# A sixth buffer for expert weights in a decoder layer's mixture of experts

## What is computed

```python
h = rmsnorm(x, norm_mix_g) * (1 + sc_a) + sh_a            # shifts, scales, gates from silu(c) @ ada_w
g_q, g_k, g_v, g_g, g_a, s_q, s_k, s_v = split(h @ w_in)   # 2320 columns
o_gla = gla_mixer(...)        # 4 heads, chunked gated linear attention
o_swa = swa_sink_mixer(...)   # 8 q / 2 kv heads, window 128, rotary, sinks
x = x + gt_a * (concat(o_gla, o_swa) @ w_out)
h = rmsnorm(x, norm_ffn_g) * (1 + sc_f) + sh_f
# router: top-1 of 4 groups, then top-2 of 8 experts inside it; 32 experts
y = sum over the two experts of weight * ((silu(h @ w_gate) * (h @ w_up)) @ w_down)   # D_EXPERT = 256
x = rmsnorm(x + gt_f * y, final_norm_g)
```

## Time and profile before

| | us |
|---|---|
| median of 3 runs | 602.33 (602.03 to 610.63) |
| the profiled execution | 603.5 |
| its span, first to last instruction | 601.6 |
| TensorE busy | 497.2 (83% of the span) |
| VectorE (DVE) busy | 272.7 (45%) |
| ScalarE (ACT) busy | 146.3 (24%) |
| GpSimd (POOL) busy | 80.4 (13%) |
| mean DMA rate over the span | 271 GB/s |

### The profile page before, as it was taken

The page is one execution under the profiler, slowest core; times in us unless marked ns, Lnnn a source line. Parts: engine busy times, 40 slices in busy tenths (PEclk is TensorE's granted clock), DMA queues, the critical chain, the costliest instruction groups (busy, mean ns, idle before and its releaser), DMA issues.

```text
span 601.6 us, 6875 instructions
## 1 busy us (share of the span) xinstructions
PE 497.2 (83%) x2596; PEld 286.6 (48%) x2596; DVE 272.7 (45%) x653; ACT 146.3 (24%) x368; POOL 80.4 (13%) x128
## 2 busy tenths in 40 slices
PE   0497999999999998999848999988898776889800
PEld 0453584646565654455545555544454443444300
DVE  4588919395665746455532623222221220222256
ACT  2402214332544532202213212111111110111111
POOL 5000000000000000012122222222212220221111
PEclk9999999999999999999958999999988898899955
DMA  8997966924500035600079999999999999999373
GB/s 295 378 354 234 352 243 215 344 71 166 114 1 1 1 115 230 285 35 36 35 268 352 382 415 415 417 413 416 415 416 417 420 416 413 416 417 373 130 288 140
DMA packets 51099, 163.10 MB, mean 271 GB/s; under 512 B 10301, under 2 KB 11342, under 8 KB 42618
## 3 DMA queue, kind: packets, MB, share of 16 engines
q1 hardware_dynamic: 40632, 151.10, 65.1%
q0 software_dynamic: 5312, 8.48, 3.8%
q10 hardware_dynamic: 5122, 3.08, 1.7%
HBM read 158.63 MB, written 12.91 MB: 285 GB/s over the span
## 4 chain that ended last, share of the span: by engine, by line
PE 59%; DMA 21%; SPq 8%; DVE 6%; issue 2%; ACT 1%; ACTq 1%; POOL 0%; POOLq 0%; DVEq 0%
PE ps L1383 19%; DMA ring<-in_w_up 17%; PE ps L1648 10%; PE ps L1562 9%; PE ps L1662 4%; SPq L458 3%; SPq L462 2%; DMA xres<-in_x 2%; SPq L459 1%; PE ps L1588 1%; ACTq L703 1%; PE ps L1640 1%; PE ps L1428 1%; PE ps L1494 1%; PE ps L1485 1%
## 5 line engine op out<-in xcount | busy, mean ns | idle before, releaser
L1383 PE MATMUL ps<-ring,hreg 128*128 128x512 f32 (+1 forms) x320 | 130.4, 562 | 2.1 <-DVE hreg L980 2.1
L1648 PE MATMUL ps<-ring,proj 128*64 128x256 f32 x336 | 87.0, 418 | 19.2 <-DMA ring<-in_w_up 18.6
L1383 PEld LDWEIGHTS ps<-ring,hreg 128*128 128x128 f32 x320 | 60.5, 193 | 62.0 <-issue 57.5
L1649 PE MATMUL ps<-ring,proj 128*64 128x256 f32 x336 | 87.0, 418 | 0.0
L1300 DVE TENSOR_TENSOR proj<-proj,ps 64x256 f32<-64x256 f32 x33 | 14.0, 423 | 159.7 <-ACT proj L880 159.7
L1648 PEld LDWEIGHTS ps<-ring,proj 128*64 128x64 f32 x336 | 48.7, 150 | 47.9 <-DMA ring<-in_w_up 19.5
L951 DVE SCALAR_TENSOR_TENSOR wide<-wide,csil 128x512 f32<-128x512 f32 x72 | 49.2, 747 | 2.3 <-DMA wide<-in_ada_w 2.2
L880 ACT ACTIVATE proj<-ps 64x256 f32<-64x256 f32 x33 | 12.4, 376 | 153.8 <-PE ps L1649 153.8
L1649 PEld LDWEIGHTS ps<-ring,proj 128*64 128x64 f32 x336 | 48.7, 150 | 0.0
L636 POOL DMA_INDIRECT y_rows<-proj,hreg x33 | 32.9, 997 | 116.0 <-DVE proj L1306 116.0
L1662 PE MATMUL ps<-ring,proj 128*64 128x512 f32 x168 | 40.2, 599 | 0.4 <-ACT proj L884 0.4
(11 more groups left out here) (277 smaller groups left out, 699.4 us busy)
## 6 DMA issues: line engine op xcount, KB each, us to landing
wide<-in_ada_w SPq DMA_DIRECT2D x24, 1024.0 KB, 8.7
ring<-in_w_gate SPq DMA_DIRECT2D x21, 1024.0 KB
ring<-in_w_up SPq DMA_DIRECT2D x21, 1024.0 KB
ring<-in_w_down SPq DMA_DIRECT2D x21, 1024.0 KB, 23.4
wide<-in_w_down SPq DMA_DIRECT2D x12, 1024.0 KB, 24.3
ring<-in_w_in SPq DMA_DIRECT2D x4, 2048.0 KB, 9.6
wide<-in_w_gate SPq DMA_DIRECT2D x6, 1024.0 KB
wide<-in_w_up SPq DMA_DIRECT2D x6, 1024.0 KB
```

The lines of the kernel that those rows point to most:

```text
L1383: mm = pe.matmul(ps[bank_of(st)][:, 0:CW[ch]], hT[:, k, b * P:(b + 1) * P], win_sb[ch][:, k, :], start=k == 0, stop=k == KD - 1)
L1648: pe.matmul(ps[bank][0:TILE, 0:F], hx[:, k, :], wg_sb[w][:, k, :], start=k == 0, stop=k == KD - 1)
L1649: mm = pe.matmul(ps[bank][TILE:P, 0:F], hx[:, k, :], wu_sb[w][:, k, :], start=k == 0, stop=k == KD - 1)
```

## The change

A sixth set of weight buffers, number 3 (`MIXED`), takes experts 3, 9, 15, 21 and 27. The former sets 3 and 4 become 4 and 5. The new set has no tensor of its own:

- gate lies in `proj` columns CQ:CV, up in CG:CA, each as 4 pieces of 512 columns (2 KB) a partition;
- down lies in `proj` columns CSK:WIN (4 pieces of 256 columns), in `gla_g` (512 columns) and in the second half of `gt_f` (512 columns), which nothing used; its load is three transfers in place of one.

Expert 3's load is issued after that of expert 2, when the four `gate_scale` and all copies of the projection are done, ahead of the wait for the output projection. Experts 4 and 5 take the places at which 3 and 4 were issued, and the loop starts at n = 6.

The working buffers make room: `heT` goes to columns CV:CG of `proj` (the mixer's result), `eo` to CSQ:CSK, the hidden values and masks to `turned`, `hg` to `spare` and to a part of `hreg`. Both last ones are in use until later than the old place was, so POOL clears them after its walk through MIXER_ORDER, behind the last squares of norm2 and the last router logits. The ids' operand `named` goes from `gla_g` to a `wa2_` of 128 rows, and `fin_g` from `spare` to `wide`, whose load waits for `e_down` of 32.

```diff
-SLOTS = 5
+SLOTS = 6
+MIXED = 3
...
-        wa2 = sb("wa2", [RANK + 1, GH * DK])
-        fin_g = spare
+        wa2_ = sb("wa2", [P, GH * DK])
+        wa2 = wa2_[0:RANK + 1, :]
+        fin_g = wide[:, 0:D]
...
+        heads = [proj[:, :, CQ:CV], proj[:, :, CG:CA]]
+        tails = [proj[:, :, CSK:WIN], gla_g[:, :], gt_f[:, D // 2:D]]
+        part += [heads]
         part += [[wide[:, a * PART:(a + 1) * PART] for a in range(3)]]
         part += [[hreg[:, 0:PART], early[:, :], wide[:, 3 * PART:4 * PART]]]
...
+        def w_cols(u, a, k):
+
+            if u == MIXED:
+                return heads[a][:, k // 2, (k % 2) * F:(k % 2 + 1) * F]
+            return part[u][a][:, k * F:(k + 1) * F]
+
+        def wd_cols(u, f, i):
+
+            if u == MIXED:
+                return tails[0][:, 2 * i:2 * i + 2, :] if f == 0 else tails[1 + i]
+            return part[u][2][:, f * D + i * PC:f * D + (i + 1) * PC]
+
+        def wd_landed(u, uses):
+            return 16 * (3 if u == MIXED else 1) * uses
...
-        named = gla_g[:, 0:8 * NE].rearrange("p (a r n) -> p a r n", a=2, r=2)
+        named = wa2_[:, 0:8 * NE].rearrange("p (a r n) -> p a r n", a=2, r=2)
...
-        hg = [take(D) for i in range(2)]
-        heT = [take(KD * P).rearrange("p (k t) -> p k t", k=KD) for i in range(2)]
-        eo = [take(D // 2) for i in range(OUTS)]
...
+        hg = [spare, hreg[:, 2 * D:3 * D]]
+        heT = [[proj[:, 2 * i + k // 4, CV + (k % 4) * P:CV + (k % 4 + 1) * P] for k in range(KD)] for i in range(2)]
+        eo = [proj[:, i, CSQ:CSK] for i in range(OUTS)]
+        sg = [turned[TILE:P, i * F:(i + 1) * F] for i in range(2)]
+        eact = [turned[0:TILE, i * F:(i + 1) * F] for i in range(2)]
+        eactT = [turned[:, (4 + i) * P:(5 + i) * P].rearrange("p (c t) -> p c t", c=FC) for i in range(2)]
...
             def gates(e, u):
-                sp.dma_start(part[u][0], gate_v[e]).then_inc(w_sem[u], 16)
-                sp.dma_start(part[u][1], up_v[e]).then_inc(w_sem[u], 16)
+                for a, src in enumerate((gate_v, up_v)):
+                    w = src[e].rearrange("p (b n) -> p b n", b=NB) if u == MIXED else src[e]
+                    sp.dma_start(part[u][a], w).then_inc(w_sem[u], 16)
 
             def downs(e, u):
-                sp.dma_start(wd_sb[u], down_v[e]).then_inc(wd_sem[u], 16)
+                if u == MIXED:
+                    sp.dma_start(tails[0], down_v[e][:, 0, :].rearrange("p (b n) -> p b n", b=NB)).then_inc(wd_sem[u], 16)
+                    for i in range(2):
+                        sp.dma_start(tails[1 + i], down_v[e][:, 1, i * PC:(i + 1) * PC]).then_inc(wd_sem[u], 16)
+                else:
+                    sp.dma_start(part[u][2].rearrange("p (k d) -> p k d", k=FC), down_v[e]).then_inc(wd_sem[u], 16)
...
             downs(2, 2)
+            sp.wait_ge(gate_scaled, NB)
+            sp.wait_ge(turn_free, len(TURN))
+            gates(MIXED, MIXED)
+            downs(MIXED, MIXED)
             sp.wait_ge(out_proj_done, 2 * NB)
...
-            gates(3, 3)
-            downs(3, 3)
-            sp.wait_ge(gath0, 16)
             gates(4, 4)
             downs(4, 4)
+            sp.wait_ge(gath0, 16)
+            gates(5, 5)
+            downs(5, 5)
...
-                    pool.wait_ge(mix_copied, NB)
-                    for i in range(2):
-                        pool.memset(hg[i], 0.0).then_inc(hg_init, 1)
...
+            pool.wait_ge(squares2, 2 * NB)
+            pool.memset(hg[0][:, :], 0.0).then_inc(hg_init, 1)
+            pool.wait_ge(logits_ready, NB)
+            pool.memset(hg[1], 0.0).then_inc(hg_init, 1)
...
-            act.wait_ge(squares2, 2 * NB)
-            act.dma_start(fin_g[:, :], final_norm_g.unsqueeze(0).broadcast_to([P, D])).then_inc(fg_in, 16)
+            act.wait_ge(e_down, NE)
+            act.dma_start(fin_g, final_norm_g.unsqueeze(0).broadcast_to([P, D])).then_inc(fg_in, 16)
```

More of the change, by code:

```diff
@@ L282, in layer_kernel @@
             sem(n) for n in ('wd_in0', 'wd_in1', 'wd_in2', 'wd_in3', 'wd_in4'))
+        w_in5, wd_in5 = (
+            sem(n) for n in ('w_in5', 'wd_in5'))
         hg_init, ids_ready, xids_in, xidx_ready = (
@@ L361, in layer_kernel @@
         xcol = rt[:, 864:864 + 4 * XT].rearrange("p (a n) -> p a n", a=4)
[L364 to L368, removed]
-        hg = [take(D) for i in range(2)]
-        heT = [take(KD * P).rearrange("p (k t) -> p k t", k=KD) for i in range(2)]
-        eo = [take(D // 2) for i in range(OUTS)]
[L372 to L377, removed]
+        hg = [spare, hreg[:, 2 * D:3 * D]]
[4 more added lines that the diff above has]
+        eactT = [turned[:, (4 + i) * P:(5 + i) * P].rearrange("p (c t) -> p c t", c=FC) for i in range(2)]
+        xmask = turned[:, 6 * P:6 * P + XT * NE].rearrange("p (t n) -> p t n", t=XT)
+        xdeep = turned[:, 10 * P:10 * P + DEEP * NE].rearrange("p (n m) -> p n m", n=NE)
+        assert XT * NE <= 4 * P and DEEP * NE <= 2 * P
         padt = shared(1, 2048, ROWS * NE // P // 2).bitcast(I32)
@@ L643, in gather_pair @@
                 if n < NE // 2:
-                    gather(gath_ids[:, n:n + 1], hg[n % 2], gath[n % 2])
+                    gather(gath_ids[:, n:n + 1], hg[n % 2][:, :], gath[n % 2])
                 else:
@@ L874, in turn @@
                 for k in range(4, KD):
-                    act.activation(heT[i][:, k, :], ps[1][:, (k - 4) * P:(k - 3) * P], ACT.Identity,
+                    act.activation(heT[i][k], ps[1][:, (k - 4) * P:(k - 3) * P], ACT.Identity,
                                    scale=amp_c[:, k:k + 1], bias=sh_c[:, k:k + 1]).then_inc(e_tokens_act, 1)
@@ L1294, in turn @@
                 for k in range(4):
-                    dve.tensor_scalar(heT[i][:, k, :], ps[0][:, k * P:(k + 1) * P], amp_c[:, k:k + 1],
+                    dve.tensor_scalar(heT[i][k], ps[0][:, k * P:(k + 1) * P], amp_c[:, k:k + 1],
                                       sh_c[:, k:k + 1], ALU.mult, ALU.add).then_inc(e_tokens_dve, 1)
@@ L1641, in turn_tile, with tokens @@
                 mm.then_inc(done, 1)
+            def tokens(i, half):
+                return [t[:, half * TILE:(half + 1) * TILE] for t in heT[i]]
             def gate_up(bank, w, hx, done, copies=0):
@@ L1662, in down_tile @@
                         mm = pe.matmul(ps[bank][i * TILE:(i + 1) * TILE, :], a[:, f, :],
-                                       wd_sb[w][:, f, 512 * i:512 * (i + 1)], start=f == 0, stop=f == FC - 1)
+                                       wd_cols(w, f, i), start=f == 0, stop=f == FC - 1)
                 mm.then_inc(done, 1)
@@ L1671, in down @@
                 pe.wait_ge(e_act_copied, n + 1)
-                pe.wait_ge(wd_sem[n % SLOTS], 16 * (n // SLOTS + 1))
+                pe.wait_ge(wd_sem[n % SLOTS], wd_landed(n % SLOTS, n // SLOTS + 1))
                 if n >= 2:
@@ L1683, in _ @@
                     pe.wait_ge(e_act, n - 1)
-                gate_up(2 + n % 2, n % SLOTS, heT[n // 2 % 2][:, :, (n % 2) * TILE:(n % 2 + 1) * TILE], e_gate_up,
-                        4 * (n // 2) + 1 if n % 2 == 0 else 0)
+                gate_up(2 + n % 2, n % SLOTS, tokens(n // 2 % 2, n % 2), e_gate_up, 4 * (n // 2) + 1 if n % 2 == 0 else 0)
                 if n % 2 and (n + 1) // 2 < NP:
@@ L1703, in _ @@
                     pe.wait_ge(w_sem[s], (m + len(range(s, NT, SLOTS))) * 32)
-                    gate_up(2 + i, s, heT[NP % 2][:, :, 0:TILE], e_gate_up)
+                    gate_up(2 + i, s, tokens(NP % 2, 0), e_gate_up)
                     pe.wait_ge(e_act, m + NT)
@@ L1708, in _ @@
                     pe.wait_ge(e_act_copied, m + NT)
-                    pe.wait_ge(wd_sem[s], (m + len(range(s, NT, SLOTS))) * 16)
+                    pe.wait_ge(wd_sem[s], (m + len(range(s, NT, SLOTS))) * wd_landed(s, 1))
                     down_tile(4 + i, s, eactT[i], e_down)
```

12 lines of the change are left out of this document (4 added, 8 removed).

## The result

| | before | changed |
|---|---|---|
| median of 20 runs each, us | 607.42 | 601.85 |
| lowest to highest, us | 601.00 to 613.22 | 597.05 to 607.56 |
| profiled execution, us (span) | 603.5 (601.6) | 604.5 (602.8) |

The ratio is 0.9926 with a 95% interval of 0.9897 to 0.9955, so the change takes off 4.5 us (2.7 to 6.3) of 607. The forecast was 3.6 us less, 598.7 against the 602.33 of the first three runs (ratio 0.994). By the bound of 2% this is no change.

What follows compares the result with a forecast made beforehand. Weight loads, slower than TensorE, were taken to bound the expert stage. Terms -7.5 (lead), +2.9 (short runs), +1.0 (clearing) and 0 (addresses) summed to -3.6 us, forecasting 598.7 from 602.33, range 594.0 to 603.5.

Steps and rivals of the forecast that it cites:

- What bounds the kernel: Expert stage: weight loads are the slower side, 7.56 us an expert against TensorE's 6.2; expert 13 waits first.
- E32: Sign at the first matmul of expert 32, the last expert: forecast to start near 558.6 us.
- Part 1 and 2: Expert weight loads: one more expert ahead, -7.5 us; shorter runs in the new slot, +2.9 us.
- load in the hole: Nearly idle load time from 254 to 303 us: expert 3's load there was taken to cost nothing.
- Part 3: Gather-buffer clearing on POOL moves behind the router logits, holds a DVE routing operation and delays the gathers: +1.0 us.
- Short runs free: Rival on the new slot's loads: short runs cost nothing, so -6.5 us, 595.8; chance 0.18.
- Tail at the low clock: Rival at the last experts: a longer wait lowers TensorE's clock, costing 1.7 us; -1.9, 600.4; chance 0.14.
- No gain at the end: Rival: the lead is not worth an expert at the end, or the stretch begins later; 602.3; chance 0.10.
- Packets dear enough to make it slower: Rival in the full stretch: new slot's packets at their upper bound, 8.3 us, give +1.8, 604.1; chance 0.08.
- The first gather was to start by 311.5: Sign after routing: a first gather starting later than 311.5 us would make the prediction wrong.
- the waits of TensorE for weights were to be under 25 us in all: Sign in the expert stage: TensorE's summed waits for weights fall under 25 us, from 29.3.
- sinking by some 10: Sign: the 415 GB/s falls by some 10 in a 30 us stretch holding expert 9, 15, 21 or 27.

Runs made afterwards that it cites:

- no bytes for expert 20: Kernel before the change, with expert 20's three weight loads cut to one partition of 128; timed ratio to the kernel before 0.9920 (0.9877 to 0.9963).
- fourth load not in the hole: Changed kernel with six slots, but expert 3's load issued after the output projection, ahead of expert 4's; ratio to the kernel before 0.9964 (0.9915 to 1.0013).
- two uses: Changed kernel with the new slot serving only experts 3 and 9; ratio to the kernel before 0.9832, or 0.9879 with ScalarE clearing the gather buffers.
- late clearing: Kernel before the change, with only the gather-buffer clearing moved to its later place, buffers left in place; ratio 1.0050 (1.0008 to 1.0092).
- short runs in ring: Changed kernel with the three weight sets in ring also cut into 2 KB and 1 KB runs; ratio to the kernel before 1.0104 (1.0056 to 1.0153).
- no bytes for expert 3: Kernel before the change, with expert 3's three weight loads cut to the first partition; ratio to the kernel before 0.9986 (0.9949 to 1.0024).

## Why the prediction was right

**What bounds the kernel** was read rightly. The first wait for weights moved from expert 13 to expert 15, in its new slot (419.99; experts "3 or 4 later" was forecast, so the lead lasts less long), E32 still waits for its weights, and fewer bytes there mean a shorter stretch (no bytes for expert 20).

**Part 1 and 2 together**: forecast -7.5 + 2.9 = -4.6, measured -5.5 to -6.0 from S to E32 in three profiles. Every profile with six slots and the old runs in the other sets has 232.0 to 233.4, and the three of the kernel before, or of it with the clearing moved or expert 3's bytes left out, 238.7 to 239.2. The mechanism is shown by three runs: bytes behind S count (expert 20), bytes ahead of S don't (expert 3), the sixth slot alone shortens the stretch (fourth load not in the hole). The premise that the load in the hole costs nothing held as well; with it elsewhere 4.1 us are lost in front of S. What each term was off by is less sure. The short runs at 8.0 ns give 4 x 1,280 x 8.0 / 16 = 2.6 instead of 2.9, which would leave 8.3 for the lead, at its upper bound of 8.4; the expert without bytes gave 6.9 and two uses instead of five 0.8, both with a tail that TensorE holds. The sum is measured, its split within 1 us is not.

**Part 3** had the right mechanism and was wrong in size twice. First, the operation that is held is the one before the one I had named, the one that was to escape. The working put 0.3 us between POOL's second table write and the clearing; the changed kernel's trace has none (308.56 + 0.97 = 309.53), and the table write itself is already in work when the operation starts at 309.07. So it is held from there to the end of both memsets: 2.34 us instead of 0.23 (1.94 in the third profile), 1.7 to 2.1 where at most 1.1 was forecast. Second, of this hardly anything reaches the first transposes, 13.8 to 14.2 us behind the logits against 13.8 in the kernel before and 14.1 in the same kernel without expert 20's bytes, because the step "it moves the gathers" left out that the gather lands behind expert 4's weights. At S it is +0.9, +0.9 and -0.2 us in the three profiles, beside a forecast of +1.0; between transposes and S lies a step of 7.7 to 7.9 or 8.4 to 8.6 us, which appears in kernels without the moved clearing too (7.9 and 8.5 in the two just named). What makes it one or the other stays open. The +1.0 was near the mark for a wrong reason.

**Sum**: -3.6 forecast; by stages from the logits to the end 299.9 - 294.7 = -5.2, timed -4.5 (-2.7 to -6.3), so the gain was larger than forecast. The range of 594.0 to 603.5 holds the median of 601.85, and a part of that is luck: the forecast stood on the 602.33 of three executions, and twenty gave 607.42. On that level the same -3.6 would have read 603.8, not 598.7. What is confirmed is the difference and not the level.

**Rivals.** Short runs free: refuted by the 11.5 us of the run with short runs in ring. Tail at the low clock: not at the last experts of the changed kernel, but there in five other runs (no bytes for expert 20, late clearing, short runs in ring and both with two uses). No gain at the end: refuted. Packets dear enough to make it slower: refuted, 8.0 ns against the 20 from which it decides.

**Signs.** Most came: the fourth load went out 52.8 us ahead of the logits, where 249 had meant 52.7; there are 6,560 packets more against 6,400; E32 lies 254.8 to 255.5 us behind the logits against 256.9 forecast; the mean rate from S to E32 is 400 and 401 GB/s against 404, under the 2%. Two did not. The first gather was to start by 311.5, that is 9.8 us behind the logits, or the prediction was wrong; it starts 10.3 to 10.7 behind them. That is the held operation again, and the time came out all the same since the gather lands no later. And the waits of TensorE for weights were to be under 25 us in all, from 29.3; they are 28.3, 29.5 and 26.0. The stage is shorter all the same, so TensorE needed less time between its waits. That fits its clock: the mean granted clock from S to E32 is 0.96, 0.96 and 0.95 in the three profiles, and 0.94 before. So the sum of the waits is a poor sign where the clock changes along with it.

The sign "sinking by some 10" was too small: two slices of the stage have 380 and 381 GB/s, where none had under 413. The changed kernel's windows show a DMA share below 1 in them:

```profile
416.00:420.00 4.00, 1.00 0.90 322
...
512.00:516.00 4.00, 1.00 0.96 364
```

## What to carry to other kernels

A buffer more is worth the bytes that it takes out of the stretch in which the transfers are full, and only those: find the event that starts that stretch. What is loaded ahead of it is worth something only if its bytes leave the stretch. An earlier issue of anything gains nothing if it then queues behind another transfer, so look for the landing. Clearing the way together with the issue brought the first transposes 1.9 us forward here; the timings don't show it yet. Where the effect is below the scatter of the spans, compare stages counted from an event inside the kernel; here the full stretch repeats within 0.5 us, where whole executions scatter by 10.

## What the runs showed of the hardware

- A 128x4 tensor_scalar of DVE that needs 0.23 us took 2.34 beside GpSimd: it began at 309.07, 0.51 us into the second table write (308.56 to 309.53), and ended at 311.41, with the second of the two memsets that follow the table write without a gap. In "late clearing" it began 0.30 us into the second memset and took 0.70. The table write alone holds it too. In "no bytes for expert 3", where no memset follows, POOL and DVE have

```profile
308.15 0.97 POOL L595 DMA_INDIRECT pair_table<-pair_i,slot_i  x1 [0.30 <-issue]
```

```profile
308.66 0.42 DVE L1196 TENSOR_SCALAR hreg<-hreg 128x4 f32<-128x4 f32 x1
```

With the copies on ScalarE in place of the memsets it took 0.23, 0.42 and 0.43 in three runs, no more than the table write explains. The Trainium skill ("SBUF — State Buffer", SBUF: two separate sides) has VectorE and GpSimd share a pair of ports under an exclusive lock, which whoever starts first gets, and ScalarE on ports of its own. The runs agree: GpSimd was in work first in each of these cases. What they add is that three GpSimd instructions in a row let the waiting one in at neither boundary.
- Packets of 1 and 2 KB cost 8 ns each beyond their bytes on one engine, all told, as "short runs in ring too" has it.
- With runs of 1 and 2 KB in the queue of the changed kernel SP's issue of one 256 KB transfer took 11.42 us, and soon behind it the DMA share fell to 0.90; the up load of expert 27 took 13.75 us to issue from 493.46 on, and the share was 0.96 from 512 to 520. The longest issue of a weight load in the full stretch is 7.62 us in the kernel before, 8.21 in "late clearing" and 6.87 with two uses, and none of these has such a dip. The dips to 380 GB/s are in all three profiles of the changed kernel. That the queue holds a number of packets, so that short ones leave it with fewer bytes, would explain it; this is argued and was not tested by itself. Behind the first of the two dips there is a rival: SP's lookup for the 33rd tile falls there (415.66 to 417.35). Behind the second there is no lookup.

```profile
401.71 11.42 SPq L480 DMA_DIRECT2D gla_g<-in_w_down  x1
```

- Waits of TensorE of 2.12 to 2.14 us ahead of expert 31 were followed by a window of four microseconds with a granted clock of 0.57 to 0.69, and one of 2.55 us in "short runs in ring too" by one of 0.57; those of 1.31 to 1.71 in the kernel before and in the changed one by windows of 1.00.
